# mLSTM operands turned by VectorE and DMA in place of TensorE, scores moved to the end of the preceding piece

## What is computed

```
s     = (q k^T) * w                     # w: gate weights, causal
num   = s v + inter * (q C)             # C: memory, 256 x 256 per head
den   = sum(s) + inter * (q n)
h     = num / max(|den|, floor)
C_new = decay * C + (w_last * k)^T v
h     = h * rsqrt(mean(h*h) + EPS) * mlstm_norm
ya    = (h * sigmoid(o)) @ w_proj_a
```

## Time and profile before

| what | value |
|---|---|
| median of 3 runs | 1900.24 us (1899.9 to 1901.29) |
| the profiled execution's own time | 1900.39 us |
| its span in the profile | 1898.6 us |
| TensorE busy | 1878.9 us (99%) |
| VectorE busy | 1348.6 us (71%) |
| ScalarE busy | 868.6 us (46%) |
| GpSimd busy | 110.3 us (6%) |
| granted TensorE clock | 0.999 of full speed |
| DMA | 126,553 packets, 272.88 MB |

### The profile page before, as it was taken

The page is one execution under the profiler, slowest core; times in us unless marked ns, Lnnn a source line. Parts: engine busy times, 40 slices in busy tenths (PEclk is TensorE's granted clock), DMA queues, the critical chain, the costliest instruction groups (busy, mean ns, idle before and its releaser), DMA issues.

```text
span 1898.6 us, 33354 instructions
## 1 busy us (share of the span) xinstructions
PE 1878.9 (99%) x13291; PEld 1854.1 (98%) x13291; DVE 1348.6 (71%) x2082; ACT 868.6 (46%) x1629; POOL 110.3 (6%) x165
## 2 busy tenths in 40 slices
PE   9999999999999999999999999999999999999997
PEld 8999999999999999999999999999999999999997
DVE  7788998999997754784455378977777776736363
ACT  5554444444554455551122355644454444635342
POOL 0011111111111111110000000000000000000000
PEclk9999999999999999999999999999999999999999
DMA  3556576666657655558131332222222223556654
GB/s 135 162 142 153 161 187 161 164 185 172 189 173 199 194 157 155 145 157 339 45 139 45 119 108 96 81 69 84 76 81 69 79 81 109 188 204 208 209 171 160
DMA packets 126553, 272.88 MB, mean 144 GB/s; under 512 B 21820, under 2 KB 61500, under 8 KB 126400
## 3 DMA queue, kind: packets, MB, share of 16 engines
q1 hardware_dynamic: 111280, 235.16, 35.8%
q0 software_dynamic: 15120, 35.59, 10.4%
HBM read 206.97 MB, written 63.74 MB: 143 GB/s over the span
## 4 chain that ended last, share of the span: by engine, by line
PE 91%; DVE 5%; DMA 2%; issue 1%; ACT 1%; SPq 0%; POOL 0%; DVEq 0%; ACTq 0%; POOLq 0%
PE ps L1202 9%; PE ps L1204 9%; PE ps L1203 9%; PE ps L1367 8%; PE ps L1368 8%; PE ps L1369 8%; PE ps L1567 7%; PE ps L1565 7%; PE ps L1566 7%; PE ps L1587 4%; PE ps L1588 4%; PE ps L1589 4%; PE ps L1295 2%; PE ps L1292 1%; PE ps L1275 1%
## 5 line engine op out<-in xcount | busy, mean ns | idle before, releaser
L1202 PE MATMUL ps<-rx,fhi 128*128 128x368 f32 (+2 forms) x736 | 248.2, 337 | 0.4 <-ACT spl L1744 0.3
L1204 PE MATMUL ps<-rx,flo 128*128 128x368 f32 (+2 forms) x736 | 237.4, 323 | 0.0
L1203 PE MATMUL ps<-rx,fhi 128*128 128x368 f32 (+2 forms) x736 | 237.1, 322 | 0.0
L1367 PE MATMUL ps<-rx,ahi 128*128 128x304 f32 (+1 forms) x672 | 194.1, 289 | 0.9 <-DVE v L2588 0.8
L1368 PE MATMUL ps<-rx,ahi 128*128 128x304 f32 (+1 forms) x672 | 193.7, 288 | 0.0
L1369 PE MATMUL ps<-rx,alo 128*128 128x304 f32 (+1 forms) x672 | 193.6, 288 | 0.0
L1587 PE MATMUL ps<-ghi,dhi 128*128 128x384 f32 (+1 forms) x528 | 173.2, 328 | 2.3 <-DVE glo L2949 1.8
L1588 PE MATMUL ps<-glo,dhi 128*128 128x384 f32 (+1 forms) x528 | 172.3, 326 | 0.0
L1589 PE MATMUL ps<-ghi,dlo 128*128 128x384 f32 (+1 forms) x528 | 172.2, 326 | 0.0
L2942 DVE TENSOR_TENSOR dlo<-draw,dhi 128x1408 fp32r<-128x1408 f32 x48 | 77.8, 1625 | 117.4 <-ACT dhi L2154 117.3
L1202 PEld LDWEIGHTS ps<-rx,fhi 128*128 128x128 f32 x736 | 138.4, 188 | 2.5 <-ACT spl L1744 1.1
(11 more groups left out here) (367 smaller groups left out, 5723.1 us busy)
## 6 DMA issues: line engine op xcount, KB each, us to landing
draw<-wdn SPq DMA_DIRECT2D x48, 704.0 KB, 4.2
araw<-wts SPq DMA_DIRECT2D x105, 256.0 KB, 4.0
uraw<-wts SPq DMA_DIRECT2D x44, 512.0 KB, 4.4
fraw<-wts SPq DMA_DIRECT2D x27, 512.0 KB, 3.6
qkv<-scr_qkv SPq DMA_DIRECT2D x22, 544.0 KB, 8.3
scr_g<-cva SPq DMA_DIRECT2D x22, 512.0 KB, 2.6
alo<-wts POOLq DMA_DIRECT2D x42, 256.0 KB, 5.2
graw<-scr_g SPq DMA_DIRECT2D x43, 192.0 KB, 4.1
```

The costliest lines, as they stand in the source:

```text
L1202: pe.matmul(b, hi[:, w], src[:, his[k], cols], start=(k == 0), stop=False)
L1203: pe.matmul(b, hi[:, w], src[:, los[k], cols], start=False, stop=False)
L1204: mm = pe.matmul(b, lo[:, w], src[:, his[k], cols], start=False, stop=(k == KB - 1))
L1367: pe.matmul(b, ahi[s][:, c], bhi[:, k, :], start=(fresh and k == 0), stop=False, skip_group_check=True)
```

## The change

1. **Keys and values** are no longer transposed by TensorE. Three pieces ahead SyncE loads 128 columns of the values (`vin`), and only k and q of a head are kept in `qkv` (four loads a head, not six). Two pieces ahead VectorE turns values and keys in blocks of 32 x 32 (`turn`, two instructions of 128 x 256). One piece ahead SyncE stores the turned blocks with four DMAs to a scratch `scr_t`, in runs of 32 numbers (128 bytes), so that the blocks stand in their places, and in piece A loads them back as `kvt` (128 rows of four runs of 512 bytes). ScalarE scales the keys in place at the start of piece A+1 (`weighted_keys`).
2. **Heads**: ScalarE scales the head into `zt` (`normed`, A+2), VectorE turns it in blocks of 32 x 32 into `zs` (`rows_out`, A+3), and SyncE stores it to `scr_z` with the tokens on the rows. The blocks get to their places when the head is reloaded: each of the eight reloads becomes four DMAs on 32 partitions each, in runs of 32 numbers (34 runs on each partition, 1,088 in each DMA).
3. **Scores** (two matmuls of q with k) of step i run at the end of piece A-1, behind the `values` of step i-2, and no longer in the middle of piece A.
4. The number per token takes two small VectorE operations in place of five (the floor is squared once at the start). The norm's gain goes into the output gate, by one more ScalarE operation of 128 x 1088 a gate tile.
5. Two of the convolution blocks change their places in `fz`, with other waits.

```diff
@@ SyncE
-                for b in range(6):
+                for b in (0, 1, 4, 5):
                     sp.dma_start(qkv[h % 2][:, b, :], scr_qkv[h, b]).then_inc(qk_in, 16)
+            def load_values(i):
+                h, j = STEPS[i]
+                if i >= 2:
+                    sp.wait_ge(turned_set, 2 * i - 3)
+                sp.dma_start(vin[i % 2][:, :, :], scr_qkv[h, 2:4, :, step_cols(j)].rearrange("b p n -> p b n"))\
+                    .then_inc(v_part_in[i % 2], 16)
+            def store_turned(i):
+                sp.wait_ge(turned_set, 2 * i + 2)
+                for a in range(4):
+                    rows = slice(32 * a, 32 * a + 32)
+                    sp.dma_start(scr_t[i][:, :, rows].rearrange("k (b n) q -> n (k b) q", n=32),
+                                 turned[i % 2][rows, :, :].rearrange("n k (b q) -> n (k b) q", q=32)).then_inc(turned_out, 16)
+            def load_turned(i):
+                if i >= 2:
+                    sp.wait_ge(n_full, i - 1)
+                sp.wait_ge(turned_out, 64 * (i + 1))
+                sp.dma_start(kvt[i % 2][:, 0:2 * DH].rearrange("n (k q) -> n k q", q=P), scr_t[i].rearrange("k n q -> n k q"))\
+                    .then_inc(kvt_in[i % 2], 16)
+            def store_head(i):
+                sp.wait_ge(zs_set, i + 1)
+                sp.dma_start(scr_z[h, step_cols(j)][first:L], zs[i % 2][first:L, :]).then_inc(z_out[i % 2], 16)
...
+                load_turned(step_at(s, 0)), store_turned(step_at(s, -1)), load_values(step_at(s, -3))
...
             for k in range(KB):
-                sp.dma_start(fx[:, KB + k, :], scr_z[k]).then_inc(blk_in[k], 16)
+                h, b = divmod(k, 2)
+                heads = scr_z[h].rearrange("(g q) (a n) -> a q g n", q=32, n=32)
+                for a in range(4):
+                    sp.dma_start(fx[32 * a:32 * a + 32, KB + k, :].rearrange("q (g n) -> q g n", n=32), heads[4 * b + a])\
+                        .then_inc(blk_in[k], 16)
@@ TensorE
-                for b in range(4):
-                    mm = pe.transpose(bank(2, b * P, P), q[:, b, cols], ident[:, :])
-                mm.then_inc(kv_full, 1)
...
-                    mm = pe.transpose(bank(3, 256 + b * L, L), zt[i % 2][:, b * P:(b + 1) * P], ident[:, :])
...
+                pe.wait_ge(kw_set, i + 1)
...
-                i = step_at(s, 3)
-                    rows_out(i)
                 i = step_at(s, 1)
                     values(i)
+                i = step_at(s, -1)
+                    scores(i)
@@ ScalarE
-                act.activation(vt[p][:, 0:DH], bank(2, DH, DH), ACT.Copy).then_inc(kv_copied, 1)
-                act.activation(kw[p][:, :], bank(2, 0, DH), ACT.Copy, scale=gt[...])
+            def weighted_keys(i):
+                act.wait_ge(kvt_in[p], 16 * (i // 2 + 1))
+                act.activation(kvt[p][:, 0:DH], kvt[p][:, 0:DH], ACT.Copy, scale=gt[...])
+            def normed(i):
+                act.wait_ge(rs_set, i + 1)
+                act.activation(zt[p][:, :], hn[p][:, 0:DH], ACT.Copy, scale=sm[p][:, 2:3]).then_inc(zt_set, 1)
@@ VectorE
+            def turn(i):
+                dve.wait_ge(v_part_in[p], 32 + 16 * (i // 2 + 1))
+                dve.transpose(turned[p][:, 2:4, :], vin[p][:, :, :]).then_inc(turned_set, 1)
+                dve.transpose(turned[p][:, 0:2, :], qkv[h % 2][:, 0:2, step_cols(j)]).then_inc(turned_set, 1)
+            def rows_out(i):
+                dve.wait_ge(zt_set, i + 1)
+                dve.transpose(zs[p][:, :], zt[p][:, :]).then_inc(zs_set, 1)
```

More of the change, by code:

```diff
@@ L94 @@
 SPL_OF = {"u": (0, 2), "g": (1, 2), "k": (1, 1), "v": (0, 0), "q": (0, 0)}
-SPL_AT = [1 + sum(sum(SPL_OF[kind]) for kind, _ in PAIRS_B[:i]) for i in range(NB + 1)]
+SPL_AT = [2 + sum(sum(SPL_OF[kind]) for kind, _ in PAIRS_B[:i]) for i in range(NB + 1)]
 V0_STORES = [[1 - p + len(range(p, min(i, NB), 2)) for i in range(NB + 2)] for p in range(2)]
@@ L203, in step_at @@
     return STEP_IN.get(NTH_FULL[s] - after)
-def rows_before(i):
-    return sum(at + 3 < STEP_AT[i] for at in STEP_AT)
-def scores_before(i):
-    return sum(at <= STEP_AT[i] + 3 for at in STEP_AT)
 def step_cols(j):
@@ L364, in batch_in @@
     n = sum(min(G_BATCH[j + 1], 21 if j == 4 else 66) - G_BATCH[j] for j in range(i % 8, i + 1, 8))
-    return i % 8, (48 if i % 8 < N_WO else 64) + 16 * n
+    return i % 8, (96 if i % 8 < N_WO else 112) + 16 * n
 EVAC_AT, evacs = [], 0
@@ L463, in build @@
     qkv = [Room(at_rz + s * 6 * blk)(f"qkv{s}", [P, 6, T]) for s in range(2)]
+    room = Room(at_rz + 2 * blk)
+    vin = [room(f"vin{s}", [P, 2, L]) for s in range(2)]
+    turned = [room(f"turned{s}", [P, 4, L]) for s in range(2)]
+    assert room.at <= at_rz + 4 * blk
     room = Room(at_rz + 6 * blk)
@@ L479, in build @@
     cb = [room(f"cb{s}", [P, 2, VW]) for s in range(2)]
-    vt = [room(f"vt{s}", [P, VW]) for s in range(2)]
-    kw = [room(f"kw{s}", [P, DH]) for s in range(2)]
+    kvt = [room(f"kvt{s}", [P, DH + VW]) for s in range(2)]
     wt = [room(f"wt{s}", [P, L]) for s in range(2)]
@@ L484, in build @@
     zt = [room(f"zt{s}", [P, DH]) for s in range(2)]
-    zs = [room(f"zs{s}", [P, 2, L]) for s in range(2)]
+    zs = [room(f"zs{s}", [P, DH]) for s in range(2)]
     nb = [room(f"nb{s}", [P, L]) for s in range(2)]
@@ L640, in build @@
         zt_set = sem("zt_set")
-        z_full = sem("z_full")
         zs_set = sem("zs_set")
@@ L797, in load_first_head @@
                 sp.wait_ge(grp_done, b_at(NB - 1, 3, 1))
-                for b in range(4):
+                for b in range(2):
                     sp.dma_start(qkv[0][:, b, :], scr_qkv[0, b]).then_inc(qk_in, 16)
@@ L861, in _ @@
             for s, ((kind, k), c) in enumerate(SLOTS):
+                i = step_at(s, 0)
+                if i is not None:
+                    load_turned(i)
+                i = step_at(s, -1)
+                if i is not None:
+                    store_turned(i)
+                i = step_at(s, -3)
+                if i is not None:
+                    load_values(i)
                 i = step_at(s, 1)
@@ L913, in _ @@
                         sp.wait_ge(spl_set, SPL_AT[NB] + m - 3)
+                    if name == "o":
+                        sp.wait_ge(spl_set, SPL_AT[NB] + 4 + m if m else 2)
                     sp.wait_ge(t_free, EVAC_AT[s - 1])
@@ L925, in _ @@
                 if i is not None:
+                    store_head(i)
+                i = step_at(s, 4)
+                if i is not None:
                     h, j = STEPS[i]
[L927 to L933 removed]
                     if j == NCHUNK:
@@ L1195, in _, with product @@
         def _(pe):
-            def product(b, hi, lo, rows, src, cols, at=0, halfway=None, his=range(KB), los=range(KB, 2 * KB)):
+            def product(b, hi, lo, rows, src, cols, his=range(KB), los=range(KB, 2 * KB)):
                 for k in range(KB):
@@ L1204, in product @@
                     mm = pe.matmul(b, lo[:, w], src[:, his[k], cols], start=False, stop=(k == KB - 1))
-                    if halfway is not None and k == at:
-                        halfway()
                 mm.then_inc(grp_done, 1)
@@ L1403, in _ @@
                             pe.wait_ge(w_acc[n % 2], 16 * NB + ACC_IN[n])
-                    i = step_at(s, 0)
-                    rows, halfway = None, (lambda: scores(i)) if i is not None else None
+                    rows = None
                     if (kind, k) == START[0]:
@@ L1416, in _ @@
                     else:
-                        product(b, fhi[wslot(n)], flo[wslot(n)], rows, rx, cols_of(s), 3, halfway)
+                        product(b, fhi[wslot(n)], flo[wslot(n)], rows, rx, cols_of(s))
                     if s == 3:
@@ L1423, in _ @@
                     gate_turn()
-                i = step_at(s, 3)
-                if i is not None:
-                    rows_out(i)
                 i = step_at(s, 1)
@@ L1429, in _ @@
                     values(i)
+                i = step_at(s, -1)
+                if i is not None:
+                    scores(i)
             pe.wait_ge(t_free, EVAC_AT[NS - 2])
-            pe.wait_ge(zs_set, 2 * len(STEPS))
+            pe.wait_ge(a_set, len(STEPS))
             pe.wait_ge(hn_set, len(STEPS))
@@ L1881, in _ @@
                     a_hi(0, 5), a_hi(0, 6), a_hi(0, 2), a_hi(0, 7), a_hi(0, 4), a_minus(0, 2), a_minus(0, 4)
+                i = step_at(s, 1)
+                if i is not None:
+                    weighted_keys(i)
                 i = step_at(s, 0)
@@ L2660, in _ @@
                     gate_columns()
+                i = step_at(s, 3)
+                if i is not None:
+                    rows_out(i)
+                i = step_at(s, -2)
+                if i is not None:
+                    turn(i)
                 i = step_at(s, 0)
```

134 lines of the change are left out of this document (63 added, 71 removed).

## The result

The changed kernel took 1953.33 us (median of 4 runs, 1951.21 to 1961.23) where the kernel before took 1900.07 on the same chip: ratio 1.0287, 95% interval 1.0258 to 1.0317. It is slower by 53 us; 1885.5 had been forecast, in a range to 1908.

What follows compares the result with a forecast made beforehand. TensorE, busy 99% of the span, was taken as the bound. From 1900.4 us: -23.0 transposes, +1.5 VectorE, +0.5 first step, 0 queue, +6.6 reload gave 1886.0, rounded down to 1885.5 us; range 1875 to 1908.

Steps and rivals of the forecast that it cites:

- The queue in the steps: SyncE's DMA cycle in the 36 steps: 6.0 us, fitting the forecast period of 6.63 us, so cost 0.
- Transposes -23.0: TensorE in the steps: removing six transposes a step saves 0.64 us each step, 23.0 us in all.
- VectorE +1.5: Steps: three block transposes replace smaller operations, mostly hidden in VectorE's idle time; 1.5 us charged, bounds 0 and 10.
- First step +0.5: First step: TensorE's next need stands behind two block transposes and two small VectorE operations; 0.5 us more, between -1 and 2.
- r = 0.85: Price of a 128-byte packet over all 16 DMA engines, in ns; taken as 0.85, near the lower row.
- Reload +6.6: After the last piece: weight tiles 3 to 5 queue behind the heads' small packets; the largest delay, 6.6 us, counts.
- Moving the scores: TensorE in the steps: moving two score matmuls from the middle of a piece to its end costs or gives nothing.
- SyncE's cycle sets the pace: Steps: a 5.5 us landing makes the cycle 7.7 us; 1930, or about 1904 at 4.5 us landing; chance 0.10.

Runs made afterwards that it cites:

- load_behind_store: Changed kernel, with SyncE issuing the next step's four stores before it waits for this step's to land: 1947.9 us.
- traffic_alone: Kernel before, with DMAs like the change's added in each step (four stores in 128-byte runs, two copies) and nothing else of it: 1952.3 us.
- traffic_tiny: Kernel before, with the same six added DMAs per step as traffic_alone, each with an eighth of its packets: 1904.6 us.
- traffic_512: traffic_alone with its four stores in runs of 512 bytes, same bytes and count of DMAs: 1911.8 us.
- long_runs: Changed kernel, with the stores of turned blocks in runs of 512 bytes, so the blocks lie in wrong places: 1936.7 us.
- light_weights: Changed kernel, with GpSimd's weight loads in the steps cut to 128 of 1024 columns: 1921.0 us.
- values_alone: Changed kernel with TensorE transposing the keys again, only values and heads turned by VectorE, head store first, load behind next stores, reload by tile: 1895.8 us.
- traffic_stores: traffic_alone without its two copies, leaving four stores in runs of 128 bytes per step: 1916.7 us.
- two_queues: Changed kernel with load behind next stores, head store first and reload by tile, plus two of four stores issued by ScalarE: 1973.1 us.
- double_turns: Kernel before, with each of its 216 TensorE transposes done twice: 1921.6 us.
- heads_alone: Changed kernel with keys and values given back to TensorE; heads' part, moved scores and reload by tile kept: 1894.7 us.
- reload_by_tile: Changed kernel, with heads reloaded one block per weight tile, each tile ahead of its block in SyncE's queue: 1940.9 us.

## Why the prediction was wrong

**The step that failed is "The queue in the steps", cost 0.** It compared SyncE's cycle (issue 0.4 + 1.8, landing 3.8 = 6.0 us) with the period and stopped there. The landing was right (3.6 us). The term that was off is the issue of the four stores: 4.4 us a step in the mean for 1.8. In the prediction's own terms the cycle is then 0.4 + 4.4 + 3.6 = 8.4 us, and the period measured is 8.43. But load_behind_store took the landing out of this cycle and the period only fell to 8.18, so that wait did not set the pace. The held issues are what stays.

What was never summed is the work of the sixteen DMA engines in a step, though all prices stood in the prediction: the share before, 0.57 of 7.27 us, is 4.1 us; 2,048 packets at the chosen 0.85 ns are 1.7; 768 packets of 512 bytes (`kvt` and `vin`) at 1.6 ns are 1.2. That is 7.1 us of work in a forecast period of 6.63: the engines would have had to be busy more than all of the time. (Two blocks fewer for each of three later heads, at 1.35 us each, take off 0.2 us a step, which leaves 6.9, still too much.) 7.2 was measured; that it is so close is partly luck. Beside that the traces show SyncE held while it issues, what stands behind it in its order (`nb`, head store, loads) late, and TensorE waiting and then at a lower clock.

The gap closes with it: the steps are 36 x (8.43 - 6.63) = 65 us over the forecast, the reload 12.4 - 6.6 = 5.8, and 2.0 had been charged for VectorE and the first step. 65 + 5.8 - 2.0 = 69, with 68 between forecast and result. No rival of the prediction named a time above 1930.

What the runs settle: transfers like the change's are enough for such a loss with nothing of its work (traffic_alone), their count is not what costs (traffic_tiny), longer runs in the stores give back 40.5 of 52 us there and some 17 of 53 in the changed kernel (traffic_512, long_runs), fewer other bytes through the same engines give back 32 (light_weights), and half the small packets cost far less than half (values_alone). What stays open: how the price of a small packet divides into the DMA engines' own time and SyncE being held at its issue. The engines' share does not order traffic_stores and traffic_512 as the times do, and the mean issue of a store, which does, may be cause or sign; the one run that gave stores to a second queue (two_queues) added a wait of its own.

Point by point:
- **Transposes -23.0**: right in kind, 21.0 by double_turns, if taking away is worth what adding costs.
- **VectorE +1.5**: a block transpose of 128 x 256 is 0.40 to 0.44 us, for 0.41 taken; VectorE was never the bound.

```profile
L2411 DVE STREAM_TRANSPOSE zs<-zt 128x256 f32<-128x256 f32 x34 | 15.0, 441 | 55.1 <-DMA scr_z<-zs 55.0
L2401 DVE STREAM_TRANSPOSE turned<-vin 128x256 f32<-128x256 f32 x36 | 14.7, 408 | 12.0 <-DMA vin<-scr_qkv 12.0
L2404 DVE STREAM_TRANSPOSE turned<-qkv 128x256 f32<-128x256 f32 x36 | 14.5, 403 | 0.0
```

- **First step +0.5**: wrong. VectorE waited 12.0 us for the values of the fourth step, whose load stood behind four stores that took 8.25 us to issue, and ScalarE 9.5 us for the first `kvt` load; TensorE did 151 matmuls in 560 to 600 us for 244. At 0.164 us each that is 15 us, which the 65 above contain.

```profile
576.34 8.25 SPq L819 DMA_DIRECT2D scr_t<-turned  x4
584.64 2.67 SPq L812 DMA_DIRECT2D vin<-scr_qkv  x1
```

- **r = 0.85**: about right. Two blocks of the reload took 10.85 us (917.04 to 927.89 on SyncE), 5.4 each; less 1.35 for its gate block, 4.07 / 4,352 = 0.94 ns. In the steps it was 0.8 (traffic_512) to 0.9 (traffic_stores: 5.9 - 4.0 = 1.9 us for 2,048).

```profile
917.04 0.69 SPq L1022 DMA_DIRECT2D fx<-scr_o  x1
917.78 4.70 SPq L1020 DMA_DIRECT2D fx<-scr_z  x4
922.51 0.59 SPq L1022 DMA_DIRECT2D fx<-scr_o  x1
...
927.89 0.61 SPq L1022 DMA_DIRECT2D fx<-scr_o  x1
928.54 0.43 SPq L714 DMA_DIRECT2D fraw<-wts  x1
```

- **Reload +6.6**: the mechanism was right, the size off. TensorE waited 8.2 us there for the low half of a tile (9.3 by the prediction's formula with 0.94 ns, for tile 5), as the row below has it, and the lower clock behind the waits brings the term to 12.4. The forecast priced the waits and not the clock.

```profile
PE ps L1243 <- DVE flo L2296: 8.2, 2, 4.1
```

- **Moving the scores**: nothing that shows, as forecast; it was not tried alone (heads_alone, which has it, met its sum within 1.1 us).
- **Rivals**: "SyncE's cycle sets the pace" named the place and the sign, with a chance of 0.10, but made it a matter of landing time (5.5 us); the landing stayed at 3.6, and load_behind_store, which takes that wait away, gave 5 us. Its second figure, 1904 for a landing of 4.5 us, does not follow from its terms: a cycle of 6.7 us against 6.63 adds 36 x 0.07 = 2.5 us at most, which gives 1900. The Trainium skill (DMA: Bandwidth & Descriptors, Specifications) says that a transfer below 512 bytes does a read-modify-write, which I had weighed only against the reload. An estimate that doubles the stores' term by it, to 3.5 us, would have shown the steps as the place; that the steps were over-full followed already without it. The runs, at 0.8 to 0.94 ns, do not show the doubling.

## What to carry to other kernels

When a change trades compute for transfers, add up the DMA engines' work in the stretch where it lands (share before times the period, plus packets times their price) and compare it with the period you hope for, before looking at any latency. No single share was the limit here: at 0.61 traffic_tiny lost 3 us, at 0.76 traffic_stores lost 15, and at 0.86 traffic_512 lost 10 and the changed kernel 53. So look beside the share at how long the issuing engine is held, in the mean and not in the median, and at what stands behind it in its order. Cut such a change into its parts: here the part with few, long runs in the hot stretch (the heads) was a gain of 6 us, and the part with runs of 128 bytes there (keys and values) lost 46 (reload_by_tile, 1940.9, against heads_alone, 1894.7). Where weights and bulk loads share an in-order queue, put the due one first: the same 34,816 packets cost 12 us in one order and nothing in the other.

## What the runs showed of the hardware

- SyncE was held while it issued a DMA with small runs behind other transfers: 0.32 us at least, 1.09 in the mean, 5.6 at most, for one store of 64 KB in 512 packets, where the median for one of 128 KB in 256 packets before was 0.37.
- Six more DMAs a step with little in them (traffic_tiny, 216 of them and an eighth of the packets) cost 3 us in all.
- A packet of 128 bytes took 0.8 ns (traffic_512) to 0.94 ns (reload) of all sixteen engines together, somewhat over half of the 1.6 ns of a packet of 512 bytes, so four of them cost about twice what the same bytes cost in one.
- TensorE's granted clock fell to 0.70 in 572 to 600 us and to 0.90 in 650 to 700 us of the changed kernel, where it had idled in pieces of up to 5 us, so a part of each wait is paid again in slower matmuls (reload: 8.2 us of waits, 12.4 us in all):

```profile
572.00:600.00 28.00, 19.98 (x76) 18.14 (x75) 14.19 (x34) 6.45 (x13) 3.72 (x5) 0.70 0.76 167
650.00:700.00 50.00, 42.07 (x224) 39.75 (x223) 32.00 (x80) 17.90 (x45) 6.14 (x10) 0.90 0.87 224
```
